# Last gate of an SSD mixer kept in the decay buffer, its transposes moved one tile back, and the squares in another order

## The chip, the cores and the metric

The kernel runs on one NeuronCore of one Trainium2 chip. The metric is the device time of one execution, in microseconds (us). The work is shared by TensorE (PE in the profile, PEld for its weight loads), VectorE (DVE), ScalarE (ACT), GpSimd (POOL) and the DMA queues, most of which SyncE (SP) issues. Each engine has its own instruction stream and runs it in order; semaphores tie them together.

## What is computed

Four layers work on 256 tokens of width 1024. A token mixer (SSD, short convolution, neighbourhood attention, SSD again) and a squared-ReLU MLP follow each other, each with a residual and a LayerNorm. The change touches the end of the two SSD mixers, cut here to what matters:

```
def grouped_rmsnorm(y, w):            # 8 groups of 256 columns
    yg = y.reshape(shp[:-1] + (SSD_GROUPS, shp[-1] // SSD_GROUPS))
    yg = yg * lax.rsqrt(jnp.mean(jnp.square(yg), axis=-1, keepdims=True) + EPS)
    return yg.reshape(shp) * w

def ssd_mixer(x, ...):
    zxbcdt = x @ w_in                 # z, x, B, C and dt
    ...
    y = y_fwd + y_bwd + d_skip[:, None] * xs
    y = y.reshape(bsz, seq, SSD_D_INNER) * jax.nn.silu(z)
    return grouped_rmsnorm(y, norm_w) @ w_out

for i in range(DEPTH):
    h = ssd_mixer(...)                # for layers 0 and 3
    x = layer_norm(alpha * x + h, ...)
    x = layer_norm(alpha * x + sq_relu_mlp(x, ...), ...)
```

## The kernel before

Weights stream from HBM in units of 128 x 2048 numbers. For each unit u, SP loads it into one of three `raw` buffers, ACT writes its rounded part to `w_high` (L1060) and DVE the remainder to `w_low` (L1447), with four buffers of each; `split_to(n)` on ACT and on DVE means "split all units up to n that are not split yet". A product is the sum of three matmuls (high by high, low by high, high by low), which gives it nearly the precision of fp32.

An SSD mixer goes through 8 groups (`G` is 8) of 256 channels. For each group there are units z, bc and x of the input projection, and a unit `so` of the output projection (256 rows of `w_out`). The last three output units of a mixer are so(5), so(6) and so(7); the next three units, fi(0) to fi(2), belong to the MLP that follows.

For one group g the chain after its projections is this. PE runs `scan` (L856), which needs the decays times C B products that DVE makes at L1624 (`decayed_products`) from the exponentials of ACT (`decays`, L1167, in two halves called early and late, four instructions each). DVE adds the two parts of y and multiplies with silu(z) into `gate` (`gate_scan`, L1668 and L1670). ACT squares `gate` (`squares`, L1196), POOL makes one over the root of the mean (`rms_power`, L473 and L474), ACT scales `gate` in place (`normalise`, L1204), PE transposes it (`turn_gated`, L867, four transposes), ACT and DVE write the transposed tile as a high and a low part to `opT` (`gated_high`, L1214; `gated_low`, L1599). Then the output unit so(g) can be multiplied (`out_part`, L711): per token tile t (two of 128) twelve matmuls of 512 columns, six for each half of the columns.

There is one `gate` buffer. So DVE may write the gate of a group only when PE has transposed that of the group before: `gate_scan` waits on `op_turned` first. The two decay buffers (`decay_slot`, halves of `E`) are used in turns, slot g % 2 for group g; after group 6 the slot 0 is not filled again in that mixer.

The order of work is written out by hand, one list for each engine. At the end of a mixer it is as follows.

- PE: scan(7); so(5) of tile 0; turn_gated(6); so(5) of tile 1; turn_gated(7); then `tail`, which does so(6) and so(7) of tile 0, then both of tile 1. After that come the transposes of the normalised tokens of tile 0 (`turn_x`, L677) and the first MLP projections (L597).
- ACT: decays(7) early and late, squares(6), tanh of z(7), normalise(6), split of so(7), gated_high(6), squares(7), normalise(7), gated_high(7), splits of fi(0) and fi(1).
- DVE: gate_scan(6), decayed_products(7), split of so(5), silu(z(7)), the terms across chunks (L1640, L1649), gate_scan(7), split of so(6), gated_low(6), split of so(7), gated_low(7), splits of fi(0) and fi(1) as one group of two, then the LayerNorm of tile 0 (`norm`, from L1474 to L1498), which ends in the tokens that `turn_x` transposes.
- POOL: the product of group 7 into `xs_own` (L446), and rms_power(6) and (7) around it.

## Time and profile before

| what | us |
|---|---|
| median of 3 runs | 1517.72 (1517.43 to 1521.18) |
| the profiled execution | 1520.08 |
| its span | 1518.2 |
| PE busy in it | 1442.0 |
| DVE busy | 997.0 |
| ACT busy | 768.2 |
| POOL busy | 196.1 |

The profiled execution is one of its own, 2.4 us above the median of the three runs; what lies around its span is 1.9 us. The mean granted clock of TensorE is 0.981 of full speed. Timeline rows give the start in us from the span's start, how long the merged instructions took from the first start to the last end, the engine, the line, the tiles, and in square brackets how long the engine had been idle before and what ended that. Where an instruction had waited for two things, the row may say only "issue". Ends of matmuls are modelled. The two mixers end at about 271 us and 1319 us; the rows are from the first one, with one of the second for comparison.

### The profile page before, as it was taken

The page shows a single profiled execution, that of the slowest core. Times are in us where ns is not written, and L with a number is a line of the kernel's source. Part 1 is how long each engine was busy: PE and PEld are TensorE (multiplying, and loading weights), DVE is VectorE, ACT ScalarE, POOL GpSimd, SP SyncE. Part 2 cuts the span into 40 slices and gives each one's busy share as a digit, 9 for nine tenths or more (in the row PEclk, how much of TensorE's full clock was granted, in tenths as well). Part 3 has the DMA queues.
Part 4 walks back from the last instruction along what each step waited for, and adds up shares of the span by engine and source line. Part 5 has one row for each costly group of instructions (what it writes and reads, how often), then busy time and mean ns, then how long its engine had stood idle before and what let it go on. Part 6 is the DMA issues. An engine that isn't in the chain of part 4 may idle for free.

```text
span 1518.2 us, 24629 instructions
## 1 busy us (share of the span) xinstructions
PE 1442.0 (95%) x9745; PEld 1331.3 (88%) x9745; DVE 997.0 (66%) x1229; ACT 768.2 (51%) x1104; POOL 196.1 (13%) x245
## 2 busy tenths in 40 slices
PE   6889998999999999999999999999989999899996
PEld 6779997898989989999899889998978999799995
DVE  3889988664567585545754465555778899864545
ACT  3678676353534335444355535443568686454441
POOL 2112322433220000000000000000113222200000
PEclk9899999999999999999999999999989999999998
DMA  7565753566666465555543246555556554446550
GB/s 212 168 194 185 232 167 113 173 195 196 207 203 210 151 213 175 193 196 194 179 157 137 84 139 200 189 188 172 151 191 194 195 172 162 152 167 208 179 209 28
DMA packets 198192, 266.96 MB, mean 176 GB/s; under 512 B 11768, under 2 KB 167824, under 8 KB 198080
## 3 DMA queue, kind: packets, MB, share of 16 engines
q1 hardware_dynamic: 188720, 237.72, 47.5%
q0 software_dynamic: 9200, 27.55, 5.9%
q8 instruction: 78, 1.28, 0.3%
q14 instruction: 34, 0.28, 0.1%
q10 hardware_dynamic: 160, 0.13, 0.0%
HBM read 264.19 MB, written 1.18 MB: 175 GB/s over the span
## 4 chain that ended last, share of the span: by engine, by line
PE 64%; DVE 6%; ACT 3%; issue 2%; DMA 1%; POOL 0%; DVEq 0%; SPq 0%; ACTq 0%; POOLq 0%
PE acc L576 28%; PE y L711 24%; PE acc L597 6%; DVE w_low L1447 2%; ACT w_high L1060 1%; PE y L597 1%; PE inner L856 1%; DMA E<-cumsum_dram 1%; PE inner L677 1%; PE y L974 0%; PE inner L954 0%; DMA raw<-in_ffn_w_out 0%; ACT xT L1090 0%; PE inner L832 0%; DVE xT L1511 0%
## 5 line engine op out<-in xcount | busy, mean ns | idle before, releaser
L576 PE MATMUL acc<-xT,w_high 128*128 128x256 f32 x3264 | 599.6, 285 | 0.0
L1447 DVE TENSOR_TENSOR w_low<-raw,w_high 128x2048 fp32r<-128x2048 f32 (+1 forms) x226 | 511.9, 2274 | 105.7 <-ACT w_high L1060 63.4
L1060 ACT ACTIVATE w_high<-raw 128x2048 fp32r<-128x2048 f32 (+1 forms) x226 | 427.2, 1896 | 206.8 <-PE y L711 77.9
L576 PEld LDWEIGHTS acc<-xT,w_high 128*128 128x128 f32 x3264 | 515.9, 193 | 4.6 <-issue 1.0
L576 PE MATMUL acc<-xT,w_low 128*128 128x256 f32 x1632 | 463.8, 284 | 0.0
L711 PE MATMUL y<-w_high,opT 128*128 128x512 f32 x1408 | 399.3, 393 | 2.8 <-DVE opT L1599 1.4
L576 PEld LDWEIGHTS acc<-xT,w_low 128*128 128x128 f32 x1632 | 315.3, 193 | 0.0
L711 PEld LDWEIGHTS y<-w_high,opT 128*128 128x128 f32 x1408 | 261.0, 189 | 55.2 <-issue 4.2
L711 PE MATMUL y<-w_low,opT 128*128 128x512 f32 x704 | 223.4, 391 | 0.0
L1466 DVE TENSOR_TENSOR opT<-conv,opT 128x512 fp32r<-128x512 f32 x56 | 38.8, 692 | 264.1 <-issue 237.2
L597 PE MATMUL acc<-w_high,xT 128*128 128x256 f32 (+1 forms) x960 | 182.3, 291 | 9.0 <-DVE xT L1511 8.7
L597 PEld LDWEIGHTS acc<-w_high,xT 128*128 128x128 f32 x960 | 154.8, 198 | 12.6 <-issue 12.3
L711 PEld LDWEIGHTS y<-w_low,opT 128*128 128x128 f32 x704 | 132.8, 189 | 28.4
L597 PE MATMUL acc<-w_low,xT 128*128 128x256 f32 (+1 forms) x480 | 138.4, 288 | 0.0
L423 POOL TENSOR_TENSOR small<-small,minus_half 128x1 f32<-128x1 f32 x16 | 15.9, 993 | 832.1 <-DVE small L1487 832.1
L1579 DVE SCALAR_TENSOR_TENSOR conv<-conv_pad,ssd_par,conv 128x256 f32<-128x256 f32 x256 | 105.6, 483 | 5.5 <-ACT conv L1134 5.5
L1103 ACT ACTIVATE conv<-acc 128x512 f32<-128x512 f32 x60 | 35.8, 597 | 143.0 <-PE acc L576 129.2
L597 PEld LDWEIGHTS acc<-w_low,xT 128*128 128x128 f32 x480 | 95.1, 198 | 0.0
L1090 ACT ACTIVATE xT<-inner 128x512 fp32r<-128x512 f32 x32 | 18.7, 597 | 109.3 <-PE inner L677 108.6
L446 POOL TENSOR_TENSOR ring_a<-ring_b,decay_to_end 128x512 f32<-128x512 f32 x16 | 33.7, 2105 | 152.7 <-ACT ring_b L1187 137.8
L1142 ACT ACTIVATE tanh<-conv 128x512 f32<-128x512 f32 x32 | 20.1, 629 | 62.4 <-DVE conv L1579 62.4
L515 POOL DMA_DIRECT2D E<-in_na_rpb x64 | 34.1, 538 | 92.8 <-ACT conv L1103 91.7
(199 smaller groups left out, 1213.4 us busy)
## 6 DMA issues: line engine op xcount, KB each, us to landing
raw<-in_ffn_w_in SPq DMA_DIRECT2D x128, 512.0 KB, 4.6
raw<-in_ffn_w_out SPq DMA_DIRECT2D x128, 512.0 KB, 4.5
raw<-in_ssd_w_in SPq DMA_DIRECT2D x96, 512.0 KB, 5.3
E<-cumsum_dram POOLq DMA_DIRECT2D x32, 512.0 KB, 6.2
raw<-in_ssd_w_out SPq DMA_DIRECT2D x32, 512.0 KB, 4.4
raw<-in_sc_w_in SPq DMA_DIRECT2D x24, 512.0 KB, 4.7
raw<-in_na_w_qkv SPq DMA_DIRECT2D x24, 512.0 KB, 4.7
raw<-in_sc_w_out SPq DMA_DIRECT2D x8, 512.0 KB, 4.4
```

The costliest lines, as they stand in the source:

```text
L446: return nc.gpsimd.tensor_tensor(spread(dst, shape), spread(tri_b[:, n % 2, :], shape), factors, ALU.mult)
L515: pool.dma_start(dst, src).then_inc(window_landed[h % WINDOW_BUFS], 16)
L576: mm = nc.tensor.matmul(bank[:, c * SEQ:(c + 1) * SEQ][:, span], w[:, col:col + P], xT[:, k, low, span], start=(k == 0 and part == 0), sto ...
L597: mm = nc.tensor.matmul(bank[:, t * width:(t + 1) * width], xT[:, k, low, t * P:(t + 1) * P], w[:, k * width:(k + 1) * width], start=(k == ...
L711: mm = nc.tensor.matmul(Y[t][c][:, :], opT[:, o % ACTS, low, k, t * P:(t + 1) * P], w[:, k * D + c * 512:k * D + (c + 1) * 512], start=(fi ...
L1060: nc.scalar.activation(w_high[:, u % SPLIT, c0:k * c], raw[:, u % RAW, c0:k * c], ACT.Copy).then_inc(w_high_done, 1)
L1090: nc.scalar.activation(xT[:, 4 * half:4 * half + 4, 0, t * P:(t + 1) * P], bank[:, :].rearrange("p (k c) -> p k c", k=4), ACT.Copy).then_i ...
L1103: nc.scalar.activation(conv[:, o % 2, :, :], views(bank[:, :]), ACT.Relu).then_inc(relu_done, 1)
L1142: nc.scalar.activation(th[:, m % 2, :], src, ACT.Tanh, scale=scale).then_inc(tanh_done, 1)
L1447: V.tensor_tensor(w_low[:, u % SPLIT, c0:k * c], raw[:, u % RAW, c0:k * c], f(w_high[:, u % SPLIT, c0:k * c]), ALU.subtract).then_inc(w_lo ...
L1466: V.tensor_tensor(low, src, high, ALU.subtract).then_inc(op_low, 1)
L1579: ins = V.scalar_tensor_tensor(out=y, in0=pad[:, c % 2, i, q:q + SEQ], scalar=tap(j, q, ct), in1=y, op0=ALU.mult, op1=ALU.add)
```

## The change

The gate of the last group of a mixer is written to the first 512 columns of decay slot 0 (`gate_of`), which group 6 used last, instead of to `gate`. With that its `gate_scan` no longer waits for the transposes of group 6. On ACT, `squares(6)` goes between the two halves of `decays(7)`, and `squares(7)` ahead of `gated_high(6)`. On PE, `turn_gated(7)` goes from before so(6) of tile 0 to behind it; the next instruction after it is so(7) of tile 0, which needs what ACT and DVE make from those transposes. Both mixers get all of this. The counts of instructions are unchanged.

```
--- before.py
+++ after.py
@@ -314,6 +314,10 @@
         y_off = flat[:, e0:e0 + 512]
         e0 += 512
         diag_out = flat[:, e0:e0 + P]
+
+        def gate_of(m):
+
+            return flat[:, (m - 1) % 2 * E_SLOT:(m - 1) % 2 * E_SLOT + 512] if m % G == G - 1 else gate[:, :]
 
         n_par_dmas = (6, (n_ssd - 1) * 6 + 1)
         out_units = [u for u, (kind, _, _) in enumerate(units) if kind in ("so", "co", "no", "fo")]
@@ -865,7 +869,7 @@
                         for c in range(2):
                             for t in range(NT):
                                 mm = nc.tensor.transpose(bank[:, c * SEQ + t * P:c * SEQ + (t + 1) * P],
-                                                         gate[:, t * GW + c * P:t * GW + (c + 1) * P], ident[:, :])
+                                                         gate_of(m)[:, t * GW + c * P:t * GW + (c + 1) * P], ident[:, :])
                         mm.then_inc(op_turned, 1)
 
                     bank = acc_bank(freed_by("bc"))
@@ -915,8 +919,8 @@
                     out_part(s, names[("so", G - 3)], o, False, False, [0])
                     turn_gated(G - 2)
                     out_part(s, names[("so", G - 3)], o, False, False, [1]).then_inc(w_used, 1)
-                    turn_gated(G - 1, ring=[("i", 0)])
-                    tail(s, [names[("so", G - 2)], names[("so", G - 1)]])
+                    tail(s, [names[("so", G - 2)], names[("so", G - 1)]],
+                         between=lambda: turn_gated(G - 1, ring=[("i", 0)]))
                     n["op"] += G
                 elif kind == "conv":
                     head_units(s, [names[("cc", 0)], names[("ch", 0)]])
@@ -1193,14 +1197,14 @@
 
                             act.wait_ge(rms_done, m)
                         for t in range(NT):
-                            ins = nc.scalar.activation(sq[:, t * GW:(t + 1) * GW], gate[:, t * GW:(t + 1) * GW],
+                            ins = nc.scalar.activation(sq[:, t * GW:(t + 1) * GW], gate_of(m)[:, t * GW:(t + 1) * GW],
                                                        ACT.Square, accum_out=small[:, 4 + t:5 + t])
                         ins.then_inc(msq_done, 1)
 
                     def normalise(g):
                         act.wait_ge(rms_done, n0 + g + 1)
                         for t in range(NT):
-                            v = gate[:, t * GW:(t + 1) * GW]
+                            v = gate_of(n0 + g)[:, t * GW:(t + 1) * GW]
                             ins = nc.scalar.activation(v, v, ACT.Copy, scale=small[:, 8 + t:9 + t])
                         ins.then_inc(scaled, 1)
 
@@ -1306,13 +1310,13 @@
                     copy_cross(G - 1)
                     copy_xs(G - 1)
                     decays(G - 1, early)
+                    squares(G - 2)
                     decays(G - 1, late)
-                    squares(G - 2)
                     z_tanh(G - 1)
                     normalise(G - 2)
                     split_to(names[("x", G - 1)] + 4)
+                    squares(G - 1)
                     gated_high(G - 2)
-                    squares(G - 1)
                     normalise(G - 1)
                     gated_high(G - 1)
                     split_to(names[("z", G - 1)] + 4)
@@ -1659,15 +1663,15 @@
                     def gate_scan(g):
 
                         m = n0 + g
-                        if g:
+                        if 0 < g < G - 1:
 
                             dve.wait_ge(op_turned, n["turned"] + 1)
                             n["turned"] += 1
                         dve.wait_ge(off_added, m + 1)
                         dve.wait_ge(yg_ready, m + 1)
-                        V.tensor_tensor(gate[:, :], y_off, inner_of[("yg", m)][:, :], ALU.add).then_inc(y_added, 1)
+                        V.tensor_tensor(gate_of(m), y_off, inner_of[("yg", m)][:, :], ALU.add).then_inc(y_added, 1)
                         dve.wait_ge(y_added, m + 1)
-                        V.scalar_tensor_tensor(out=gate[:, :], in0=gate[:, :], scalar=0.5, in1=tri_c[:, m % 3, :],
+                        V.scalar_tensor_tensor(out=gate_of(m), in0=gate_of(m), scalar=0.5, in1=tri_c[:, m % 3, :],
                                                op0=ALU.mult, op1=ALU.mult).then_inc(gated, 1)
 
                     def silu_z(g):
@@ -1788,7 +1792,7 @@
                     gated_low(G - 1)
                     split_to(names[("z", G - 1)] + 4)
                     n["op"] += G
-                    n["turned"] += 1
+                    n["turned"] += 2
                 elif kind == "conv":
                     for b in range(4):
                         o = n["op"]
```

PE at the end of the first mixer. Before, the second L867 row (group 7) stands behind so(5) of tile 1 and ahead of so(6) of tile 0:

```order
L711 MATMUL y<-w_high,opT 128x512 x2
L867 MATMUL inner<-ident,gate 128x128 x4
L711 MATMUL y<-w_high,opT 128x512 x2
L711 MATMUL y<-w_low,opT 128x512 x2
L711 MATMUL y<-w_high,opT 128x512 x4
L711 MATMUL y<-w_low,opT 128x512 x2
L711 MATMUL y<-w_high,opT 128x512 x2
L867 MATMUL inner<-ident,gate 128x128 x4
L711 MATMUL y<-w_high,opT 128x512 x2
L711 MATMUL y<-w_low,opT 128x512 x2
L711 MATMUL y<-w_high,opT 128x512 x4
L711 MATMUL y<-w_low,opT 128x512 x2
```

After the change (all lines are four higher, L871 is `turn_gated`), the same place:

```order
L871 MATMUL inner<-ident,gate 128x128 x4
L715 MATMUL y<-w_high,opT 128x512 x2
L715 MATMUL y<-w_low,opT 128x512 x2
L715 MATMUL y<-w_high,opT 128x512 x4
L715 MATMUL y<-w_low,opT 128x512 x2
L715 MATMUL y<-w_high,opT 128x512 x4
L715 MATMUL y<-w_low,opT 128x512 x2
L715 MATMUL y<-w_high,opT 128x512 x4
L715 MATMUL y<-w_low,opT 128x512 x2
L715 MATMUL y<-w_high,opT 128x512 x2
L871 MATMUL inner<-ident,E 128x128 x4
L715 MATMUL y<-w_high,opT 128x512
```

The four transposes of group 7 now read `E` and stand twelve matmuls later, directly ahead of the first matmul of so(7).

ACT at the end of the first mixer, from the decays of group 7 (L1167) to the splits of fi(0) and fi(1). Before:

```order
L1167 ACTIVATE E<-E,neg_cumsum 128x128 x8
L1196 ACTIVATE square,small<-gate 128x256 x2
L1142 ACTIVATE tanh<-acc 128x512
L1204 ACTIVATE gate<-gate,small 128x256 x2
L1060 ACTIVATE w_high<-raw 128x2048
L1214 ACTIVATE opT<-inner,ssd_par 128x256 x2
L1196 ACTIVATE square,small<-gate 128x256 x2
L1204 ACTIVATE gate<-gate,small 128x256 x2
L1214 ACTIVATE opT<-inner,ssd_par 128x256 x2
L1060 ACTIVATE w_high<-raw 128x2048 x2
```

After:

```order
L1171 ACTIVATE E<-E,neg_cumsum 128x128 x4
L1200 ACTIVATE square,small<-gate 128x256 x2
L1171 ACTIVATE E<-E,neg_cumsum 128x128 x4
L1146 ACTIVATE tanh<-acc 128x512
L1208 ACTIVATE gate<-gate,small 128x256 x2
L1064 ACTIVATE w_high<-raw 128x2048
L1200 ACTIVATE square,small<-E 128x256 x2
L1218 ACTIVATE opT<-inner,ssd_par 128x256 x2
L1208 ACTIVATE E<-E,small 128x256 x2
L1218 ACTIVATE opT<-inner,ssd_par 128x256 x2
L1064 ACTIVATE w_high<-raw 128x2048 x2
```

The squares of group 6 now cut the decays of group 7 in two, those of group 7 stand ahead of `gated_high(6)`, and the two splits (L1064 x2) still stand last, behind `gated_high(7)`. DVE, POOL and SP keep their order; on DVE only the wait of the last `gate_scan` on `op_turned` is gone.

## Rows read from the trace of the kernel before

**Rows 1.** The page, busy time of each engine: us, share, instructions.

```profile
PE 1442.0 (95%) x9745; PEld 1331.3 (88%) x9745; DVE 997.0 (66%) x1229; ACT 768.2 (51%) x1104; POOL 196.1 (13%) x245
```

**Rows 2.** Timeline of PE, end of the first mixer: start, length, instructions, idle before.

```profile
246.76 2.00 PE L856 MATMUL inner<-ring_b,E 128*128 128x64 f32 x16 [0.61 <-DVE E L1624]
249.27 0.70 PE L711 MATMUL y<-w_high,opT 128*128 128x512 f32 x2 [0.52 <-issue]
...
252.12 0.60 PE L867 MATMUL inner<-ident,gate 128*128 128x128 f32 x4
...
254.84 0.61 PE L711 MATMUL y<-w_high,opT 128*128 128x512 f32 x2
258.18 1.06 PE L867 MATMUL inner<-ident,gate 128*128 128x128 f32 x4 [2.72 <-ACT gate L1204]
...
262.58 0.85 PE L711 MATMUL y<-w_high,opT 128*128 128x512 f32 x3
...
270.98 0.39 PE L711 MATMUL y<-w_high,opT 128*128 128x512 f32 x1
271.61 1.32 PE L677 MATMUL inner<-ident,x_tokens 128*128 128x128 f32 x8 [0.24 <-DVE x_tokens L1498]
```

**Rows 3.** Timeline of DVE, the same stretch.

```profile
243.56 1.16 DVE L1670 SCALAR_TENSOR_TENSOR gate<-gate,ring_c 128x512 f32<-128x512 f32 x1
...
245.49 1.22 DVE L1624 TENSOR_TENSOR E<-E,acc 128x1024 f32<-128x1024 f32 x1 [0.23 <-ACT E L1167]
...
246.89 2.28 DVE L1447 TENSOR_TENSOR w_low<-raw,w_high 128x2048 fp32r<-128x2048 f32 x1
...
252.75 0.69 DVE L1668 TENSOR_TENSOR gate<-E,inner 128x512 f32<-128x512 f32 x1 [1.65 <-PE inner L867]
...
256.28 0.87 DVE L1599 SCALAR_TENSOR_TENSOR opT<-inner,ssd_par,opT 128x256 fp32r<-128x256 f32 x2
...
260.15 0.88 DVE L1599 SCALAR_TENSOR_TENSOR opT<-inner,ssd_par,opT 128x256 fp32r<-128x256 f32 x2 [0.64 <-ACT opT L1214]
262.01 4.49 DVE L1447 TENSOR_TENSOR w_low<-raw,w_high 128x2048 fp32r<-128x2048 f32 x2 [0.98 <-issue]
266.42 0.68 DVE L1474 SCALAR_TENSOR_TENSOR x_tokens<-x_tokens,y 128x512 f32<-128x512 f32 x1
```

**Rows 4.** Timeline of ACT, the same stretch.

```profile
243.00 2.46 ACT L1167 ACTIVATE E<-E,neg_cumsum 128x128 f32<-128x128 f32 x8
245.36 0.40 ACT L1196 ACTIVATE square<-gate 128x256 f32<-128x256 f32 x1
...
246.16 0.57 ACT L1142 ACTIVATE tanh<-acc 128x512 f32<-128x512 f32 x1
...
259.28 0.84 ACT L1214 ACTIVATE opT<-inner,ssd_par 128x256 fp32r<-128x256 f32 x2 [1.15 <-PE inner L867]
260.01 3.71 ACT L1060 ACTIVATE w_high<-raw 128x2048 fp32r<-128x2048 f32 x2
```

**Rows 5.** Timeline of DVE, then of POOL, group 5 at 207 us.

```profile
207.11 2.28 DVE L1447 TENSOR_TENSOR w_low<-raw,w_high 128x2048 fp32r<-128x2048 f32 x1
...
207.27 3.03 POOL L446 TENSOR_TENSOR ring_b<-ring_b,own_token 128x512 f32<-128x512 f32 x1 [1.71 <-DVE own_token L1630]
```

**Rows 6.** Stretches: us, busy (instructions) of PE, PEld, DVE, ACT, POOL, granted clock, DMA.

```profile
258.35:261.76 3.41, 3.41 (x11) 2.83 (x11) 2.04 (x3) 2.48 (x3) 0.00 (x0) 0.51 0.99 333
...
746.40:749.80 3.40, 3.40 (x17) 3.40 (x18) 2.24 (x2) 3.40 (x3) 0.00 (x0) 0.50 0.81 300
...
466.50:470.00 3.50, 2.65 (x21) 2.30 (x20) 1.61 (x4) 3.25 (x4) 1.15 (x2) 1.00 0.49 171
```

**Rows 7.** Timeline of PE, transposes of normalised tokens at two other norms.

```profile
744.11 1.32 PE L677 MATMUL inner<-ident,x_tokens 128*128 128x128 f32 x8 [1.06 <-DVE x_tokens L1498]
...
465.99 1.32 PE L677 MATMUL inner<-ident,x_tokens 128*128 128x128 f32 x8 [1.50 <-DVE x_tokens L1498]
```

**Rows 8.** Timeline of PE, the second mixer's transposes of its last gate.

```profile
1306.05 1.04 PE L867 MATMUL inner<-ident,gate 128*128 128x128 f32 x4 [2.72 <-ACT gate L1204]
```

More of the change, by code:

```diff
@@ L316, in build, with gate_of @@
         diag_out = flat[:, e0:e0 + P]
+        def gate_of(m):
+            return flat[:, (m - 1) % 2 * E_SLOT:(m - 1) % 2 * E_SLOT + 512] if m % G == G - 1 else gate[:, :]
         n_par_dmas = (6, (n_ssd - 1) * 6 + 1)
@@ L867, in turn_gated @@
                                 mm = nc.tensor.transpose(bank[:, c * SEQ + t * P:c * SEQ + (t + 1) * P],
-                                                         gate[:, t * GW + c * P:t * GW + (c + 1) * P], ident[:, :])
+                                                         gate_of(m)[:, t * GW + c * P:t * GW + (c + 1) * P], ident[:, :])
                         mm.then_inc(op_turned, 1)
@@ L917, in _ @@
                     out_part(s, names[("so", G - 3)], o, False, False, [1]).then_inc(w_used, 1)
-                    turn_gated(G - 1, ring=[("i", 0)])
-                    tail(s, [names[("so", G - 2)], names[("so", G - 1)]])
+                    tail(s, [names[("so", G - 2)], names[("so", G - 1)]],
+                         between=lambda: turn_gated(G - 1, ring=[("i", 0)]))
                     n["op"] += G
@@ L1195, in squares @@
                         for t in range(NT):
-                            ins = nc.scalar.activation(sq[:, t * GW:(t + 1) * GW], gate[:, t * GW:(t + 1) * GW],
+                            ins = nc.scalar.activation(sq[:, t * GW:(t + 1) * GW], gate_of(m)[:, t * GW:(t + 1) * GW],
                                                        ACT.Square, accum_out=small[:, 4 + t:5 + t])
@@ L1202, in normalise @@
                         for t in range(NT):
-                            v = gate[:, t * GW:(t + 1) * GW]
+                            v = gate_of(n0 + g)[:, t * GW:(t + 1) * GW]
                             ins = nc.scalar.activation(v, v, ACT.Copy, scale=small[:, 8 + t:9 + t])
@@ L1308, in _ @@
                     decays(G - 1, early)
+                    squares(G - 2)
                     decays(G - 1, late)
-                    squares(G - 2)
                     z_tanh(G - 1)
@@ L1313, in _ @@
                     split_to(names[("x", G - 1)] + 4)
+                    squares(G - 1)
                     gated_high(G - 2)
-                    squares(G - 1)
                     normalise(G - 1)
@@ L1661, in gate_scan @@
                         m = n0 + g
-                        if g:
+                        if 0 < g < G - 1:
                             dve.wait_ge(op_turned, n["turned"] + 1)
@@ L1667, in gate_scan @@
                         dve.wait_ge(yg_ready, m + 1)
-                        V.tensor_tensor(gate[:, :], y_off, inner_of[("yg", m)][:, :], ALU.add).then_inc(y_added, 1)
+                        V.tensor_tensor(gate_of(m), y_off, inner_of[("yg", m)][:, :], ALU.add).then_inc(y_added, 1)
                         dve.wait_ge(y_added, m + 1)
-                        V.scalar_tensor_tensor(out=gate[:, :], in0=gate[:, :], scalar=0.5, in1=tri_c[:, m % 3, :],
+                        V.scalar_tensor_tensor(out=gate_of(m), in0=gate_of(m), scalar=0.5, in1=tri_c[:, m % 3, :],
                                                op0=ALU.mult, op1=ALU.mult).then_inc(gated, 1)
@@ L1790, in _ @@
                     n["op"] += G
-                    n["turned"] += 1
+                    n["turned"] += 2
                 elif kind == "conv":
```

## The prediction

> **What bounds the kernel now.** I read the page first: PE is busy for 1442.0 of 1518.2 us [rows 1], so what counts is where PE stands still, or runs at a lower clock, and whether that reaches the next stage. Then the timeline of PE at the end of a mixer. Its largest hole there is 2.72 us ahead of the transposes of group 7 at 258.18, ended by ACT's normalise; the second mixer shows the same 2.72 us [rows 2, 8]. After it the granted clock is at the lower of its two levels (0.51 of full, 1.2 GHz) from 258.35 for 3.41 us, with PE busy throughout [rows 6]. That is the price that meets the eye: 2.72 us, and half of 3.41, 1.7 us. Together 4.4 us per mixer, 8.8 us in all.
>
> Next the question of what comes out at the other end of the tail. PE's last output matmul starts at 270.98 and lasts 0.39, so PE is done at 271.37; the token transposes start at 271.61, after 0.24 us of idle time that the LayerNorm on DVE ended [rows 2]. So PE and the norm end almost together, and both have to be followed. The norm starts at 266.42 [rows 3]. By PE it could have started sooner: the half of tile 0 that it reads first is done eight matmuls into what starts at 262.58, at about 264.5 [rows 2]. It starts where the two splits of fi(0) and fi(1) end on DVE, 262.01 + 4.49 [rows 3]. Those follow ACT's rounding of the same units, which starts at 260.01, and this stands in ACT's list behind the copy of the transposes of group 7 at 259.28, which starts when those transposes end on PE [rows 4]. **The chain to the next stage is: transposes of group 7, ACT copy, two roundings, two splits, norm, token transposes.** Its first link is what the change moves. The norm follows the end of those transposes by a fixed 7.1 us (259.28 to 266.42).
>
> **The squares of group 6 inside the decays of group 7.** The eight exponentials start at 243.00 and take 2.46 us, so the early four end at about 244.2. The squares need the gate of group 6, which is written at 243.56 + 1.16 = 244.72 [rows 3]. ACT stands for 0.5 us, does the squares in 0.8 us (245.36 to 246.16) [rows 4], and ends the late four at about 246.8 in place of 245.5: 1.3 us later. DVE's product of group 7 starts at 245.49, having idled for 0.23 us for just those exponentials [rows 3], so it moves by 1.3 us. Behind it on DVE is queued the split of so(5), from 246.89 to 249.17. PE's scan(7) waited 0.61 us for the product, and so(5) starts at 249.27, where the split ends [rows 2, 3]. Nothing covers this: scan(7) goes to 248.1 and so(5) to 250.6. What the squares gain is nothing, since PE reaches the transposes of group 6 at 252.12 without a wait [rows 2].
>
> **The gate in the decay buffer.** gate_scan(7) starts at 252.75 after 1.65 us of waiting for the transposes of group 6 [rows 3]. Without that wait it could start at 251.10; with DVE 1.3 us late it starts at 252.4. So 0.35 us is gained, not 1.65. The rest of this chain took 5.43 us from there to the transposes of group 7 (252.75 to 258.18) [rows 2, 3], so the scaled gate is ready at 257.8, or 258.7 if the copy of group 6 (0.8 us), which now stands between squares and normalise, is added in full.
>
> **The transposes behind so(6) of tile 0.** so(5) of both tiles with the transposes of group 6 between ran from 249.27 to 255.45 (254.84 + 0.61) [rows 2]; now it ends at 256.8. so(6) needs DVE's part of group 6, which ended at 256.28 + 0.87 = 257.15 and comes 0.35 us sooner, at 256.8 [rows 3]: no new hole. The pitch of one matmul is 0.227 us (from the first of the group at 262.58 to 270.98 there are 37 steps) [rows 2], so twelve take 2.7 us and the transposes of group 7 start at 259.5. The scaled gate has been there for 0.8 us or more: the 2.72 us hole is gone. At full clock the transposes take 0.60 us [rows 2] and end at 260.1. Before they ended at 259.24 (258.18 + 1.06, partly at the low clock). **The first link of the chain is 0.9 us later**, and with it the copy, both roundings, both splits and the norm, since all of these are queued behind it. That is +1.8 us for two mixers.
>
> Meanwhile PE waits after the transposes, for so(7) needs both parts of group 7. DVE's part ended at 261.03, 1.75 us after ACT's copy began [rows 3, 4]; now 261.9. From there 36 matmuls take 8.2 us, and PE is done at 270.2 or 270.3, 1.1 us sooner than before. This gain meets no one: the token transposes wait for the norm, now until 272.5. The 0.24 us of idle time grows to 2.3 us. The hole is not removed but moved to behind the tail.
>
> **The clock after that hole.** The low stretch from 258.35 goes; before, it cost the chain only the slower transposes, as PE had time in hand. Behind the moved hole come the transposes, a short wait, and the MLP's projections, where time lost is lost for good. Other norms bound the price. At 744.11 a hole of 1.06 us ahead of the same eight transposes was followed by the low clock (0.50) from 746.40 for 3.4 us under projections: 1.7 us. At 465.99 a hole of 1.50 us was followed by none, full clock to 470 [rows 6, 7]. So 0 to 1.7 us per mixer, 0 to 3.4 in all, and not below nothing, as this place is at full clock before. The hole of 2.3 us is larger than both, but a low stretch can also lie on the hole or the short wait. I take 1.2 us for both mixers together, about a third of the upper end.
>
> **A port that could turn this.** At 207 us POOL's product with own_token and DVE's split of 2048 columns come at once: DVE starts 0.16 us ahead and takes its usual 2.28, POOL takes 3.03 and ends 0.9 us after it [rows 5]. The same pair meets at the end of group 7, and there the delay of DVE changes the start: POOL was busy with the power of group 6 before and is free now. By the order at 207 us DVE stays first, POOL ends about 0.3 us before its result is wanted, and the sum is unchanged. The Trainium skill (SBUF — State Buffer, "SBUF: two separate sides") says that GpSimd and a VectorE operation with two SBUF inputs share a port pair, and that whichever starts first keeps it for the whole instruction while the other waits. The trace agrees with POOL as the loser. By that rule the sum would be larger if POOL came first.
>
> **The sum.** +1.8 for the chain and +1.2 for the clock: +3.0 us. On the profiled execution of 1520.08 that gives 1523.1. It lies 2.4 us above the median of the runs (1517.72), and since both share the tails I add the 3.0 to the median: 1520.7 us, 0.2% more.
>
> **The rivals.**
> - The clock falls under the projections in both mixers. Place: the first MLP projections after the hole; price 1.7 each; 1.8 + 3.4 = +5.2, 1522.9 us, slower. For it: 744 us, with a smaller hole. Against: 466 us. It decides from a loss of 2.8 us in both together. Chance 0.20.
> - POOL takes the port first. The split of so(5) starts 0.9 to 1.0 us later, and with it everything behind it, twice: about +5.0, 1522.7 us, slower. For it: POOL now waits idle for DVE's signal. Against: 207 us. Chance 0.05.
> - The norm does not hang on the splits after all, and the token transposes follow PE's earlier end: 1.1 us less per mixer, 1515.5 us. For it: only 0.24 us of idle time separates the two ends. Against: the norm starts where the splits end. Chance 0.12.
> - The whole hole and its low clock come back: 4.4 us twice, 1508.9 us. It needs squares and decays to cost nothing and the norm to start early. Chance 0.05.
> - The edit does nothing measurable: the 0.9 us is lost in the readings from which I put it together (each good to 0.1 or 0.2 us) or in where low-clock stretches fall elsewhere; 1517.7 us. Chance 0.13.
> - The forecast: 0.45.
>
> **How the numbers follow.** About 0.3% (4.6 us) is what a measurement of this kernel can tell from no change. Forecast, "norm does not hang" and "nothing measurable" lie within it: 0.45 + 0.12 + 0.13 = 0.70. Slower by more: 0.20 + 0.05 = 0.25. Faster by more: 0.05. The range runs from just below 1515.5 to just above 1522.9, with 0.7 us for the spread of a median: 1515.2 to 1523.6; it leaves out the last of the faster cases and little else.
>
> **What the profile after would show.** Chain: DVE's product of group 7 starts 1.3 us later than 245.49, and so(5) at about 250.6. Gate: DVE's first gate instruction of group 7 with no wait for PE, near 252.4. Move: PE's transposes of group 7 at about 259.5 with no hole ahead, a hole of about 1.8 us behind, ACT's two roundings at 260.9, the norm at 267.3. End: token transposes at 272.5 after about 2.3 us of idle time. The prediction is wrong if the norm starts at 266.4 or sooner, if so(5) still starts at 249.3, or if the last hole is under 1 us.

## The result, and the profile after

The changed kernel takes 1524.04 us (median of 9 runs, 1518.71 to 1527.35) where the kernel before takes 1517.38 (9 runs, 1515.05 to 1521.18). The ratio is 1.0043, with a 95% interval of 1.0031 to 1.0055: slower by 6.5 us (4.7 to 8.3). The forecast was 1520.7 and a range up to 1523.6; its sign was right, its size (3.0 us) less than half of what came, and the measured time lies outside the range.

The profiled executions hide this. The one after has a span only 1.9 us longer:

```profile
span 1520.1 us, 24629 instructions
...
PE 1439.3 (95%) x9745; PEld 1330.2 (88%) x9745; DVE 998.1 (66%) x1229; ACT 767.3 (50%) x1104; POOL 196.7 (13%) x245
```

So the tails have to be compared themselves. The whole trace after runs 0.42 us ahead up to there; a mark that no part of the change moves is the start of the second gate instruction of group 6 on DVE, 243.56 before [rows 3] and 243.14 after. All distances below are from this mark. The timeline of PE after (columns as in [rows 2]; line numbers are four higher):

```profile
247.72 2.00 PE L860 MATMUL inner<-ring_b,E 128*128 128x64 f32 x16 [1.98 <-DVE E L1628]
250.23 0.70 PE L715 MATMUL y<-w_high,opT 128*128 128x512 f32 x2 [0.52 <-issue]
...
253.08 0.60 PE L871 MATMUL inner<-ident,gate 128*128 128x128 f32 x4
...
256.64 0.70 PE L715 MATMUL y<-w_high,opT 128*128 128x512 f32 x2 [0.21 <-DVE opT L1603]
...
259.49 0.60 PE L871 MATMUL inner<-ident,E 128*128 128x128 f32 x4
262.02 0.47 PE L715 MATMUL y<-w_high,opT 128*128 128x512 f32 x1 [1.93 <-DVE opT L1603]
...
270.05 0.39 PE L715 MATMUL y<-w_high,opT 128*128 128x512 f32 x1
272.46 1.32 PE L681 MATMUL inner<-ident,x_tokens 128*128 128x128 f32 x8 [2.02 <-DVE x_tokens L1502]
274.62 0.55 PE L601 MATMUL acc<-w_high,xT 128*128 128x256 f32 x2 [0.84 <-DVE xT L1515]
...
286.93 0.48 PE L601 MATMUL acc<-w_high,xT 128*128 128x256 f32 x2 [1.07 <-DVE xT L1515]
```

DVE and then ACT, the same stretch (these answer to [rows 3, 4]):

```profile
243.14 1.16 DVE L1674 SCALAR_TENSOR_TENSOR gate<-gate,ring_c 128x512 f32<-128x512 f32 x1
...
246.44 1.22 DVE L1628 TENSOR_TENSOR E<-E,acc 128x1024 f32<-128x1024 f32 x1 [1.60 <-ACT E L1171]
...
252.09 0.69 DVE L1672 TENSOR_TENSOR E<-E,inner 128x512 f32<-128x512 f32 x1
...
262.85 4.50 DVE L1451 TENSOR_TENSOR w_low<-raw,w_high 128x2048 fp32r<-128x2048 f32 x2 [0.98 <-issue]
267.26 0.68 DVE L1478 SCALAR_TENSOR_TENSOR x_tokens<-x_tokens,y 128x512 f32<-128x512 f32 x1
```

```profile
244.33 0.42 ACT L1200 ACTIVATE square<-gate 128x256 f32<-128x256 f32 x1 [0.48 <-DVE gate L1674]
...
260.12 0.84 ACT L1218 ACTIVATE opT<-inner,ssd_par 128x256 fp32r<-128x256 f32 x2 [2.65 <-PE inner L871]
260.85 3.71 ACT L1064 ACTIVATE w_high<-raw 128x2048 fp32r<-128x2048 f32 x2
```

The hole of 2.72 us is gone. In its place PE has three: 1.98 us ahead of scan(7) (0.61 before), 1.93 ahead of so(7), 2.02 ahead of the token transposes (0.24 before). From the mark, the product of group 7 is 1.37 us later (3.30 against 1.93), so(5) 1.38 (7.09 against 5.71), the copy of group 7 on ACT 1.26 (16.98 against 15.72), the norm 1.26 (24.12 against 22.86) and the token transposes 1.27 (29.32 against 28.05). The second mixer shows the same to 0.05 us (token transposes 29.35 from its mark against 28.03). Up to here the trace is the forecast with 1.27 where 0.9 was written. Then the clock. The stretches of the trace after (us, PE busy, granted clock, DMA):

```profile
247.72:251.10 3.38, 2.86 (x20) 1.00 0.00 0
274.90:278.30 3.40, 3.40 (x18) 0.50 0.03 7
1322.80:1326.20 3.40, 3.40 (x18) 0.50 0.00 0
```

In both mixers TensorE runs at the lower level (1.2 GHz) for 3.4 us under the first MLP projections, and by the projections after the transposes of tile 1 (286.93) the delay has grown to 2.33 us (43.79 from the mark; before they stand at 285.02, 41.46 from it). In the second mixer it is 2.36 us (43.80 against 41.44). The two tails are 4.7 us, still short of 6.5.

### The profile page after: what moved, and what is told of

Its sections match the earlier page's. It is cut to its first block, busy times and chain, and to the rows that moved or that the text cites. A ratio compares the mean times of both kernels' runs of the same rounds, so it can differ in the third digit from the quotient of the medians.

```text
span 1520.1 us, 24629 instructions
## 1 busy us (share of the span) xinstructions
PE 1439.3 (95%) x9745; PEld 1330.2 (88%) x9745; DVE 998.1 (66%) x1229; ACT 767.3 (50%) x1104; POOL 196.7 (13%) x245
## 3 DMA queue, kind: packets, MB, share of 16 engines
q8 instruction: 78, 1.28, 0.3%
## 4 chain that ended last, share of the span: by engine, by line
PE 81%; DVE 9%; ACT 4%; issue 3%; DMA 2%; SPq 0%; DVEq 0%; POOL 0%; ACTq 0%
PE acc L580 36%; PE y L715 28%; PE acc L601 9%; DVE w_low L1451 3%; PE y L601 2%; ACT w_high L1064 2%; DMA E<-cumsum_dram 1%; PE inner L860 1%; DVE conv L1583 1%; PE inner L836 1%; DMA raw<-in_ssd_w_in 1%; PE inner L681 1%; PE inner L825 1%; ACT E L1161 1%; DMA raw<-in_na_w_qkv 1%
## 5 line engine op out<-in xcount | busy, mean ns | idle before, releaser
L1064 ACT ACTIVATE w_high<-raw 128x2048 fp32r<-128x2048 f32 (+1 forms) x226 | 427.2, 1896 | 190.0 <-PE y L715 88.7
L601 PE MATMUL acc<-w_high,xT 128*128 128x256 f32 (+1 forms) x960 | 186.1, 296 | 9.6 <-DVE xT L1515 9.1
L601 PEld LDWEIGHTS acc<-w_high,xT 128*128 128x128 f32 x960 | 158.1, 203 | 13.2 <-issue 12.9
```

The source lines that it names most:

```text
L601: mm = nc.tensor.matmul(bank[:, t * width:(t + 1) * width], xT[:, k, low, t * P:(t + 1) * P], w[:, k * width:(k + 1) * width], start=(k == ...
L1064: nc.scalar.activation(w_high[:, u % SPLIT, c0:k * c], raw[:, u % RAW, c0:k * c], ACT.Copy).then_inc(w_high_done, 1)
```

## Experiments

Changes are against the kernel before from the same chip and hour; intervals are of the ratio, and a change in us is the ratio's. The ratio is not the quotient of the two medians; where the medians say something else by half a us or more, both are given. "The cut" is the squares of group 6 between the two halves of the decays of group 7, "the move" the transposes of group 7 behind so(6) of tile 0, "the gate" the decay buffer together with the earlier squares of group 7. A profile is one execution, and the rows shown are from the first mixer unless they start after 1280 us.

**Undo the cut in the decays.** From the changed kernel:

```
                     decays(G - 1, early)
-                    squares(G - 2)
                     decays(G - 1, late)
+                    squares(G - 2)
```

> The changed kernel with one part undone: the squares of group 6 stand again behind all eight decays of group 7 (the gate in the decay buffer, the early squares of group 7 and the transposes behind so(6) of tile 0 stay). Theory A (the next stage hangs on the chain transposes of group 7, copy, two roundings, two splits, norm; plus the low clock after the hole behind the tail): DVE's product of group 7 is 1.3 us earlier again, so(5) starts where it did before, the transposes of group 7 end at about 259.0 instead of 259.24 before, the norm starts 0.2 us earlier than before, and a hole of about 2.1 us stays ahead of the token transposes. Time: 0.4 us under before, plus 0 to 3.4 us for the clock: 1517 to 1520.5. Rival C (the moved transposes alone cost the time, the cut in the decays costs nothing): as the changed kernel, 1524.

Measured: 1518.55 beside 1517.99, ratio 1.0006 (0.9993 to 1.0018). PE of this kernel:

```profile
256.80 0.60 PE L871 MATMUL inner<-ident,E 128*128 128x128 f32 x4
259.33 0.47 PE L715 MATMUL y<-w_high,opT 128*128 128x512 f32 x1 [1.93 <-DVE opT L1603]
...
269.78 1.32 PE L681 MATMUL inner<-ident,x_tokens 128*128 128x128 f32 x8 [0.43 <-DVE x_tokens L1502]
```

Its mark is at 241.83, so the token transposes are 27.95 behind it against 28.05. With the cut gone the loss is gone; rival C is out. One detail was wrong: no hole of 2.1 us stands ahead of the token transposes but one of 0.43. In this execution PE ran at half speed under so(7) and what follows, and was done later for it:

```profile
260.00:263.40 3.40, 3.40 (x10) 0.51 0.18 63
1304.50:1307.90 3.40, 3.40 (x10) 0.50 0.32 96
```

The second row is the same place in the second mixer. Here the hole ahead of scan(7) is as short as before, and the clock fell in both tails just behind the hole of 1.93 us ahead of so(7). It cost the next stage nothing: the projections after tile 1 start 41.35 and 41.33 from the marks, against 41.46 and 41.44 before.

**The cut alone.** From the kernel before:

```
                     decays(G - 1, early)
-                    decays(G - 1, late)
                     squares(G - 2)
+                    decays(G - 1, late)
```

> The kernel before with one part of the change alone: the squares of group 6 between the two halves of the decays of group 7. Theory A: everything from DVE's product of group 7 on moves by 1.3 to 1.4 us, up to the norm and the token transposes; the holes of 2.72 us and 0.24 us stay as they were, so no new low-clock stretch: 2 x 1.35 = +2.7 us, 1520.1. Rival C (the cut costs nothing, the split of the squares is hidden in PE's hole of 2.72 us): 1517.4, with that hole 1.3 us smaller.

Measured: 1522.62 beside 1517.99, ratio 1.0033 (1.0022 to 1.0044), which is 5.0 us and clearly over the 2.7 of theory A. The profile shows what A had left out. PE, and the stretch from 249.5:

```profile
249.36 3.55 PE L856 MATMUL inner<-ring_b,E 128*128 128x64 f32 x16 [1.98 <-DVE E L1624]
...
276.78 1.32 PE L677 MATMUL inner<-ident,x_tokens 128*128 128x128 f32 x8 [0.36 <-DVE x_tokens L1498]
```

```profile
249.50:256.40 6.90, 6.90 (x25) 0.51 0.46 152
```

The hole ahead of scan(7) is 1.98 us, as in the changed kernel, and here the clock falls at its end, for 6.9 us, over scan(7) and nearly all of so(5) of tile 0. The mark is at 244.75, so the token transposes are 32.03 behind it, 4.0 us more than before. The second mixer has the same hole of 1.98 us and no low stretch, and its token transposes are 1.0 us later than before. I formed theory A2: the new hole ahead of scan(7) also lets the clock fall, in some executions, and what is lost there lies on the chain.

**The gate alone.** The changed kernel with the cut and the move undone (squares(7) stays ahead of `gated_high(6)`):

```
-                    tail(s, [names[("so", G - 2)], names[("so", G - 1)]],
-                         between=lambda: turn_gated(G - 1, ring=[("i", 0)]))
+                    turn_gated(G - 1, ring=[("i", 0)])
+                    tail(s, [names[("so", G - 2)], names[("so", G - 1)]])
...
                     decays(G - 1, early)
-                    squares(G - 2)
                     decays(G - 1, late)
+                    squares(G - 2)
```

> The changed kernel with two parts undone: squares of group 6 behind the decays as before, transposes of group 7 ahead of so(6) as before. What is left is the gate of group 7 in the decay buffer and its squares ahead of the copy of group 6. Theory A: gate 7 starts 1.65 us earlier (251.1 by the clock of the trace before), the transposes of group 7 at about 256.5 after a hole of 1.0 us instead of 2.72, the norm and the token transposes about 2.1 us earlier; per mixer -2.1, with a hole of about 1.7 us ahead of the token transposes that can cost 0 to 1.7 in clock: 1513.2 to 1516.6. Rival B (PE's own path counts, not the norm): PE's tail ends 3.5 us earlier and so does the next stage, 1510.4.

Measured: 1515.75 beside 1517.99, ratio 0.9986 (0.9977 to 0.9995): 2.1 us faster. Token transposes 26.18 from the mark (244.46), 1.87 less than before:

```profile
257.67 0.60 PE L871 MATMUL inner<-ident,E 128*128 128x128 f32 x4
...
270.64 1.32 PE L681 MATMUL inner<-ident,x_tokens 128*128 128x128 f32 x8 [1.47 <-DVE x_tokens L1502]
```

One thing spoke ahead for the next step: under so(5) this execution, too, has the clock low, though its hole ahead of scan(7) is only 0.61 us as before:

```profile
249.90:253.40 3.50, 3.23 (x8) 0.51 0.59 184
1314.90:1318.30 3.40, 3.32 (x15) 0.50 0.00 0
```

PE's tail waits 1.47 us for the norm, so the norm is what counts, not PE's path (rival B). In the second mixer the token transposes come 1.99 us sooner than before (26.04 against 28.03), but behind its hole of 1.47 us the clock falls under the projections (the second row) and takes half of that back, so this execution gains 2.8 us in its two tails and not 3.9. This part of the change is good. The three parts by these ratios: gate -2.1; cut +5.0 (alone, on the kernel before); move +3.0 (undo the cut, less the gate alone). They sum to 5.9, beside 6.5 for all; each is good to some 2 us, so this does not show that they simply add.

**Fill the last hole.** From the changed kernel, behind the tail (the wait for the bank `A[k]` is left out here):

```
+                    for q in range(8):
+                        nc.tensor.matmul(A[k][:, :], opT[:, (o + 2) % ACTS, 0, 1, P:2 * P],
+                                         w_high[:, names[("so", G - 1)] % SPLIT, D:D + 512], start=True, stop=True)
```

> The changed kernel with eight matmuls of 512 columns added on PE at the end of each SSD tail, behind so(7) of tile 1 and ahead of the token transposes, into a bank that the next projection overwrites. They compute nothing that is used; they fill about 1.8 of the 2.0 us hole there. Theory A with the clock as a large part: no timestamps ahead of the token transposes change, but the low-clock stretch under the first projections of the MLP is gone in both mixers; 1.7 us less for each, 1520.6 to 1521.5. Rival D (the clock has no part, the whole +6.6 us is waits): 1524 or a little more.

Measured: 1523.82 beside 1517.99, ratio 1.0037 (1.0023 to 1.0052): 5.6 us against 6.5 of the changed kernel. The intervals overlap, and the expected 2.5 to 3.4 us did not come back. Its profile has no low clock under the MLP's first projections, but from scan(7) on in the first mixer, and under so(5) and so(7) in the second:

```profile
248.80:255.70 6.90, 6.90 (x23) 0.51 0.45 152
1300.10:1303.60 3.50, 3.50 (x10) 0.51 0.78 258
1313.80:1317.20 3.40, 3.40 (x10) 0.50 0.08 21
```

The added matmuls have a cost of their own. They take PE's spare time ahead of the norm, so the slow so(7) of the second mixer reaches the token transposes: they come 31.68 from the mark (1292.56), where a second look at the changed kernel, below, has the same two low stretches and 30.43. Taken alone this run would say that the last hole is the smaller part. It shows neither that nor rival D, as the clock was low elsewhere.

**Fill all three holes.** The same lines, seven matmuls of that kind in `between` behind the transposes of group 7, and eight ahead of scan(7):

```
-                    scan(G - 1)
+                    scan(G - 1, 8)
...
+                        bank = inner_bank(("yg", m), (y_added, m + 1), ring=[("i", 0)])
+                        for q in range(fill):
+                            nc.tensor.matmul(bank[:, :], xT[:, KT - 1, 0, 0:P], w_high[:, names[("z", G - 1)] % SPLIT, 0:512],
+                                             start=True, stop=True)
                         pe.wait_ge(g_done, m + 1)
                         pe.wait_ge(xs_copied, m + 1)
-                        bank = inner_bank(("yg", m), (y_added, m + 1), ring=[("i", 0)])
```

> The changed kernel with all three of its holes per SSD tail filled with matmuls of 512 columns that compute nothing used: eight ahead of scan(7) (hole of 1.98 us), seven ahead of so(7) of tile 0 (1.93 us), eight ahead of the token transposes (2.02 us). Theory A2 (waits plus a clock that falls at any of these holes, not only at the last): all time stamps of the chain as in the changed kernel, no low-clock stretch from scan(7) to the MLP's first projections, so only the chain is left: 2 x 1.26 = +2.5 us over the kernel before, 1520.5. Rival D (clock has no part; filling the last hole alone gave 1523.8): again 1523 to 1524.

Measured: 1520.97 beside 1517.42, ratio 1.0020 (1.0007 to 1.0033), 3.0 us (3.6 by the medians); theory A2's 2.5 is within the interval. The profile is the cleanest of all: full clock over both tails, and the chain where the changed kernel has it. Stretches, then PE:

```profile
240.00:290.00 50.00, 45.33 (x271) 1.00 0.43 146
1289.00:1336.00 47.00, 42.32 (x247) 1.00 0.43 139
```

```profile
273.13 1.32 PE L681 MATMUL inner<-ident,x_tokens 128*128 128x128 f32 x8 [0.19 <-DVE x_tokens L1523]
```

The token transposes stand 29.33 behind the mark (243.80), as in the changed kernel (29.32). So what is left with the clock held is 1.28 us per mixer (1.30 in the second), and the rest of the 6.5 us, 3.5 us by the ratios of two occasions, is put down to the clock.

**The cut alone, with the hole ahead of scan(7) filled.** The scan lines just shown, on the kernel of the cut alone.

> The kernel before with the squares of group 6 inside the decays of group 7 (as in e2_squares_only) and eight matmuls that compute nothing used in the hole of 1.98 us ahead of scan(7). Theory A2: the low-clock stretch of 6.8 us that e2's profile shows from scan(7) on does not come; what is left is the shift of the chain, 2 x 1.35 = +2.7 us: 1520.7 beside 1518.0. Rival D: the 4.6 us of e2_squares_only are all waits, again 1522.6.

Measured: 1519.38 beside 1517.42, ratio 1.0009 (0.9999 to 1.0020): 1.4 us in place of 5.0 (2.0 and 4.6 by the medians). From 247 on, where the cut alone was low, this kernel has full clock:

```profile
247.00:257.00 10.00, 8.51 (x46) 1.00 0.32 105
```

The clock is low later, from 258.4 near the end of the hole of 2.73 us, much as in the kernel before, and in the second mixer under the projections. The added matmuls compute nothing that is used and give 3 us or so back. The intervals of the two kernels, each against the kernel before of its own occasion, do not meet, if only just (up to 1.0020, and from 1.0022); rival D is out.

**The gate alone, with one rounding off the chain.**

```
                     gated_high(G - 2)
+                    split_to(names[("z", G - 1)] + 4)
                     normalise(G - 1)
```

> The kernel e3_gate_only (gate of group 7 in the decay buffer and its squares early, nothing else of the change), with ACT's rounding of fi(0) moved ahead of its normalise of group 7, into the idle time there. Theory A (the norm hangs on the roundings and splits behind the copy of group 7): the normalise and the transposes of group 7 come 0.7 us later, but one rounding of 1.8 us is off the chain; the norm starts 1.1 us sooner than in e3 and the hole of 1.47 us ahead of the token transposes nearly closes; 2 x 0.7 to 1.1 us and less low clock: 1513 to 1514.5. Rival B (PE's path counts): 0.7 us later per mixer than e3, 1517.

Measured: 1513.68 beside 1517.42, ratio 0.9975 (0.9961 to 0.9989), 3.8 us faster, the lowest ratio here. ACT:

```profile
253.05 1.91 ACT L1064 ACTIVATE w_high<-raw 128x2048 fp32r<-128x2048 f32 x1
...
258.71 1.92 ACT L1064 ACTIVATE w_high<-raw 128x2048 fp32r<-128x2048 f32 x1 [1.36 <-DMA raw<-in_ffn_w_in]
...
1301.29 1.91 ACT L1064 ACTIVATE w_high<-raw 128x2048 fp32r<-128x2048 f32 x1 [0.72 <-DMA raw<-in_ffn_w_in]
```

The rounding of fi(0) now lies in ACT's idle time, but that of fi(1) then waits 1.36 us for its data. So the token transposes come 25.83 from the mark (268.12 less 242.29), 0.35 less than with the gate alone and not 0.7 to 1.1. The next bound in this tail is a transfer. In the second mixer the rounding of fi(0) itself waits 0.72 us for its data (the last row) and holds up the normalise behind it; PE was at half speed under so(6) as well, and the token transposes come 27.18 from the mark, 1.1 later than with the gate alone. What both tails do show is the chain: from ACT's copy of group 7 to the norm it is 7.14 us with the gate alone and here 6.42 and 6.06. That this kernel is faster than the gate alone is not shown: the intervals overlap, and its profile gains 2.3 us in the two tails and that one 2.8. The 1.7 us between this kernel and the gate alone is a difference of two ratios from different occasions.

**The kernel before with its hole filled.** Eleven matmuls of the same kind ahead of `turn_gated(G - 1)`.

> The kernel before with eleven matmuls that compute nothing used in its hole of 2.72 us ahead of the transposes of group 7. Theory A (the low clock that follows that hole costs the chain only the slower transposes): transposes in 0.6 instead of 1.06 us, PE done 1.7 us earlier but waiting for the norm: 0.3 to 0.9 us under before, 1517.1 to 1517.7. Rival (the low stretch there costs its full 1.7 us per mixer): 1514.6.

Measured: 1517.34 beside 1517.42, ratio 1.0002 (0.9987 to 1.0016). The profile:

```profile
257.99 0.66 PE L867 MATMUL inner<-ident,gate 128*128 128x128 f32 x4 [0.24 <-ACT gate L1210]
...
271.02 1.32 PE L677 MATMUL inner<-ident,x_tokens 128*128 128x128 f32 x8 [1.46 <-DVE x_tokens L1504]
```

Full clock through both tails, and the token transposes come only 0.41 us sooner (27.64 from the mark at 243.38, against 28.05), which the quicker transposes of group 7 give; the measured time cannot tell 0.8 us from nothing. PE is done sooner and stands 1.46 us for the norm. So the 3.4 us of low clock in the kernel before were nearly free. This run does not price the hole itself, for the wait for the scaled gate stays; the gate alone starts those transposes 1.4 and 1.6 us sooner in the two tails, and gains by it.

**The changed kernel with the hole ahead of scan(7) filled.** The scan lines shown above, nothing else.

> The changed kernel with only its hole ahead of scan(7) filled, by eight matmuls that compute nothing used; the other two holes stay. With the last hole alone filled the loss was 5.8 us, with all three 3.5. Theory A2 with most of the clock at scan(7): about 2 to 2.5 us under the changed kernel, a loss of 4 to 4.5 us, 1521.5 to 1522. Rival (most of the clock is lost behind the last hole, as the changed kernel's own profile suggests): a loss of 5.5 us or more, 1523 to 1524.

Measured: 1522.51 beside 1520.59 (on this occasion the kernel before was slower too), ratio 1.0020 (1.0007 to 1.0032): 3.0 us of loss in place of 6.5 (1.9 and 6.7 by the medians). The gain of 3.5 us is more than the 2 to 2.5 expected, but the intervals of the two kernels touch (up to 1.0032, and from 1.0031). The stretch there is at full clock, while the low one under the MLP's first projections stays:

```profile
247.00:262.00 15.00, 12.46 (x64) 1.00 0.52 166
275.40:278.80 3.40, 3.40 (x18) 0.50 0.03 7
1323.30:1326.70 3.40, 3.40 (x18) 0.50 0.00 0
```

**A second look at the changed kernel.** No edit.

> The changed kernel as it is, for a second profile. Theory A2: the same holes (1.98, 1.93 and 2.0 us) at the same places to 0.1 us in each mixer, but the low-clock stretches may lie elsewhere: of four tails in two profiles at least one is expected with a stretch from scan(7) on instead of, or beside, the one under the MLP's first projections. Rival (the stretches are fixed to the kernel): again only behind the last hole, in both mixers.

One execution, 1527.98 us, longer than any of the nine in the result. PE, then the stretches:

```profile
249.01 2.94 PE L860 MATMUL inner<-ring_b,E 128*128 128x64 f32 x16 [1.99 <-DVE E L1628]
...
256.85 0.60 PE L871 MATMUL inner<-ident,gate 128*128 128x128 f32 x4
...
1327.35 1.32 PE L681 MATMUL inner<-ident,x_tokens 128*128 128x128 f32 x8 [0.38 <-DVE x_tokens L1502]
```

```profile
249.90:256.70 6.80, 6.80 (x22) 0.50 0.46 154
277.20:284.00 6.80, 6.11 (x28) 0.50 0.13 31
1304.60:1308.00 3.40, 3.40 (x10) 0.50 0.81 259
1318.20:1321.60 3.40, 3.40 (x10) 0.50 0.08 19
```

The same instructions, and a clock that falls elsewhere: 13.6 us at half speed in this first tail, where the first profile has 3.4. The three holes of this tail are equal to 0.01 us; in the second tail the last one is 0.38 and not 2.01, against what was expected, as PE was slow under so(7) and done later. From the start of scan(7) to the transposes of group 6 it takes 7.84 us (249.01 to 256.85) and took 5.36 (247.72 to 253.08): 2.5 us. This is the loss ahead of so(6) that the first profile of the changed kernel does not contain; 2.0 us of it reach the norm (26.12 from the mark against 24.12), and 1.1 in the second mixer (25.23).

**The tails of all profiles side by side.** How much later than in the kernel before the projections after the transposes of tile 1 start, from the mark of each mixer, in us; beside it the change of the whole time by the ratio.

| kernel | first tail | second tail | both | measured |
|---|---|---|---|---|
| changed | +2.33 | +2.36 | +4.7 | +6.5 |
| changed, second look | +5.50 | +2.40 | +7.9 | |
| cut undone | -0.11 | -0.11 | -0.2 | +0.9 |
| cut alone | +3.98 | +1.04 | +5.0 | +5.0 |
| gate alone | -1.87 | -0.97 | -2.8 | -2.1 |
| last hole filled | +3.26 | +3.41 | +6.7 | +5.6 |
| all three holes filled | +1.27 | +1.30 | +2.6 | +3.0 |
| cut alone, hole ahead of scan(7) filled | +1.45 | +2.07 | +3.5 | +1.4 |
| gate alone, rounding moved | -1.17 | -1.09 | -2.3 | -3.8 |
| before, hole filled | -0.41 | -0.40 | -0.8 | +0.3 |
| changed, hole ahead of scan(7) filled | +2.32 | +2.34 | +4.7 | +3.0 |

The four tails of the changed kernel come to 3.15 us each, 6.3 for an execution, beside the 6.5 measured: the tails account for the loss. For the other kernels the two tails of the one profile and the measured change differ by up to 2.1 us.

## Why the prediction was half right

- **What bounds the tail: right.** The norm starts 7.14 us behind ACT's copy of group 7, before and after (267.26 less 260.12), and with one rounding moved off that chain it was 6.42 and 6.06. PE's own path, with its 4.4 us of apparent loss, was not what counted: with full clock over the tail of the kernel before, PE stood 1.46 us for the norm and the time stayed at 1.0002.
- **The cut in the decays: right in place and size.** ACT stood 0.48 us (0.5 forecast), the product and so(5) moved by 1.37 and 1.38 us (1.3).
- **The gate: right.** gate_scan(7) starts 8.95 from the mark instead of 9.19, 0.24 sooner (0.35), and does not wait for PE. DVE also stayed ahead of POOL where the two meet: DVE's split of so(5) starts at 247.85, POOL's product behind it takes 3.03 us as at 207 us (2.81 before at this place, where it came 0.38 us behind DVE), from

```profile
248.01 3.03 POOL L450 TENSOR_TENSOR ring_b<-ring_b,own_token 128x512 f32<-128x512 f32 x1 [1.72 <-DVE own_token L1634]
```

  to 251.04. The rule of the Trainium skill that was weighed (SBUF — State Buffer, "SBUF: two separate sides": whichever starts first keeps the shared port pair) agrees with that.
- **The move: right in kind, mis-sized.** The transposes of group 7 ended 1.27 us later, not 0.9. Two terms were off. "No new hole" ahead of so(6): there is one of 0.21 us, since DVE's part of group 6 ended at 256.49 and PE started 0.15 behind it, so that so(6) began 0.26 us later than written (256.64, which is 257.06 by the times before, against 256.8). "Twelve take 2.7 us": from 256.64 to the transposes at 259.49 it is 2.85, as for the twelve of so(5) from 249.27 to 252.12 in [rows 2]. The hole behind them, 1.93 (1.8), and the last one, 2.02 (2.3), came. Two tails cost 2.5 us, not 1.8.
- **The clock: the step that failed.** The forecast priced a fall only behind the last hole, 1.2 us in all. By its own terms the hole ahead of scan(7) grows from 0.61 to 1.9 us, and it put no price on that beyond the wait. The runs show a price. By the cut alone and its filled twin it is 3.6 us (5.0 less 1.4); by the changed kernel with that one hole filled, 3.5 us (6.5 less 3.0). Both are differences of ratios from two occasions, each good to some 2.3 us; by the medians they are 2.7 and 4.7. The profiles give less: a fall there came in 5 of 8 tails and brought the norm 2.5, 2.0, 2.0, 1.1 and 1.1 us later, which is 2.2 us per execution. There the lost time is on the chain, since so(5) and the transposes of group 6 are slow and so(6) and the transposes of group 7 stand in line behind them.
- **The last hole's fall: right in kind, too low.** The clock fell under the projections in all five tails that have this hole of 2.0 us unfilled (both of the first profile, the first of the second look, both with only the hole ahead of scan(7) filled), and in 2 of the 6 where it is 1.44 to 1.47 us. A stretch of 3.4 us cost 1.04 to 1.06 us (in the first profile 2.33 less 1.27), so about 2.1 us for two mixers and not 1.2; the stretch of 6.8 us in the second look cost 2.24, over the 1.7 given as the upper end. Filling this hole alone changed the time by less than the runs can tell, with the clock lower elsewhere and PE's spare time gone. Which of the two places weighs more is not settled.
- **The rivals.** "Slower, the clock falls in both mixers" had the right outcome and part of the cause, at 1522.9 and 0.20: it lacked the fall at scan(7). "The whole hole comes back", "the norm does not hang on the splits" and "nothing measurable" fell, and so did "POOL takes the port first": DVE was 0.16 us ahead of it in both mixers.

The hole of 1.93 us ahead of so(7) is the third place: the clock fell behind it in 4 of the 10 tails that have it, twice with nothing longer than 0.61 us ahead of scan(7) (the cut undone), and there it cost nothing, for PE is done about 2 us ahead of the norm. Left open: how often each fall comes over many executions, since a profile is one, and with that how the 3.5 to 4 us of clock divide between scan(7) and the last hole.

## What to carry to other kernels

Do not take the longest hole of the busiest engine, and the low clock behind it, for the loss: follow the chain to the next stage and find what stands in line behind each link. A slow stretch on an engine that will wait for another anyway is free, as here behind the hole of 2.72 us; the same stretch on the chain is not. When a change makes a hole longer, price it twice, once as a wait and once as a fall of the TensorE clock over the matmuls behind it, and ask of each hole apart whether those matmuls are on the chain. Splitting a run of instructions to let another engine's result in early only pays if that result is waited for; here the squares gained nothing, and the four decays behind them held up everything.

## What the runs showed of the hardware

- The same program shows its low-clock stretches at other places from one execution to the next: 3.4 us in the first tail of one profile and 13.6 us in another, with the three holes of that tail equal to 0.01 us. The executions of one kernel spread by 4 to 10 us (the changed one from 1518.71 at a mean granted clock of 0.984 to 1527.35 at 0.975), so one profile does not bound what a hole costs.
- Counted over all profiles, a low stretch lay over scan(7) or so(5) in 5 of the 8 tails with the hole of 1.98 us ahead of scan(7) (one of two with the cut alone, both with the last hole filled, none of two and both of two in the looks at the changed kernel), in 1 of the 10 tails with the hole of about 0.6 us, and in none of the 6 where the longer hole was filled. In three of them it lasted 6.8 or 6.9 us.
- Eight matmuls that compute nothing, put into that hole, made the kernel of the cut alone 3 us or so faster (3.6 by the ratios, 2.7 by the medians), with no instruction on any other engine changed.
